# Two transformer blocks in float32 on one core: an altered matmul order at the start of the FFN down projections

## The chip, the cores and the metric
The kernel runs on one core of a Trainium2 chip. The core has a tensor engine (PE in the profile; its weight loads are PEld), a vector engine (DVE), a scalar engine (ACT), GpSimd (POOL) and SyncE (SP), which here only starts DMA transfers. The engines run their own instruction streams and wait for each other on semaphores. The metric is the device time of one execution in microseconds, as the median of several runs.

## The reference
An input of 256 tokens by 1024 features (272 tokens with 16 meta tokens in front) goes through a block of two layers (latent attention, then window pooling, each followed by a convolutional feed-forward network) and then through a second block (gated linear attention and convolution, a gated feed-forward network, an extra gate, a last norm). There are three feed-forward networks; each has an up projection and a down projection with 2816 hidden features between them:

```python
def conv_ffn(h, w_up, conv_w, conv_b, w_down):        # first block, layers 0 and 1
    L = h.shape[1]
    u = h @ w_up
    up = jnp.pad(u, ((0, 0), (CONV_WIDTH - 1, 0), (0, 0)))
    u = conv_b + sum(conv_w[j] * up[:, j:j + L] for j in range(CONV_WIDTH))
    gate, val = jnp.split(u, 2, axis=-1)
    return (jax.nn.silu(gate) * val) @ w_down
...
        a, bb = jnp.split(u2 @ w_gate_upffn[i], 2, axis=-1)   # second block
        h = h + (jax.nn.silu(a) * bb) @ w_down[i]
```

## The kernel before, in words
Every product in float32 is made of three matmuls on a high and a low part of both operands (`three`, lines 379 to 381: high by high, high by low, low by high). So each weight tile has to be split first: ACT copies `raw` to `w_high` with rounding (L752 for a first half, L755 for the rest or the whole), then DVE and POOL each subtract for their columns of `w_low` (DVE L1083 and L1088, POOL L1575, which has a quarter of the columns or a little more).

Weights come in **units**. A unit of a down projection holds the 22 tiles of 128 rows (chunks 0 to 21) that make one block of 128 output features: 22 x 3 = 66 matmuls into one PSUM bank, with 272 tokens in the first network and 256 in the other two. A down projection has eight units, 0 to 7; each network's units are called unit 0, unit 1 and so on below (`n0`, `n0 + 1` in the code). There are two slots of `raw`, `w_high` and `w_low`, so unit n+2 uses the slots of unit n: ACT may write `w_high` of unit n+2 only when PE has finished unit n (it waits for `products`), while SP may load `raw` of unit n+2 as soon as unit n has been split. In program order ACT does, after unit n's last matmul, in the first two networks the square (L771) and the copy (L796) of its output (`post`), then the high part of unit n+2 (`high`); in the third network the high part comes first. DVE and POOL follow with the low parts, and PE waits for all three counters before unit n+2 (`parts_ready`).

The moving operand of chunk k, `x_high` and `x_low`, is made during the up projection from its turn k: scaling from PSUM, convolution taps, SiLU, product, then ACT L805 (`x_high`) and DVE L1188 (`x_low`). In the first two networks the work of a turn is finished one turn later, so the last two chunks, 20 and 21, are finished after the up projection's last matmul. PE waits for each chunk of unit 0 by name (`x_ready`). Unit 1 follows unit 0; its x is the same, so it waits for no chunk. Units 2 to 7 run in a loop.

The order of the work is the order in which the code is written, engine by engine; there is no scheduler.

Of the kernel before, what the change touches and what calls it, by code (L numbers as in the profile page):

```python
# [50 lines left out]
FC = FF // P  # L51
# [69 lines left out]
FIRST_UNIT, FIRST_BLOCK, UNITS, BLOCKS = {}, {}, [], []  # L121
# [46 lines left out]
def program(nc, dram, marks, final):  # L168
    ctx = ExitStack()
    with ctx:  # L170
        def sb(name, shape, dt=F32, stack=None):
            return (stack or ctx).enter_context(nc.sbuf_tensor(name, shape, dt))

        def sem(name):
            return ctx.enter_context(nc.semaphore(name))
# [3 lines left out]
        def done(name, i=None):  # L179


            engine, n, loop = marks.get(name, ("scalar", 1, None))
            stride = marks.get(("stride", engine, loop), 1)
            if final and name not in marks:
                raise KeyError(name)
            if isinstance(i, tuple):
                i, n = i[0], n - i[1] * stride
            return step_sems[engine], n if i is None else i * stride + n

        products = sem("products")  # L190
# [40 lines left out]
        xh = sb("x_high", [P, FC, T1], F32R)  # L231
        xl = sb("x_low", [P, FC, T1], F32R)
# [33 lines left out]
        bank = [ctx.enter_context(nc.psum_tensor(f"bank{b}", [P, 512], F32)) for b in range(8)]  # L266
# [74 lines left out]
        def up_place(j):  # L341


            return (j, None) if j < 2 or j >= FC - 2 else (f"k{j % 2}", (j - 2) // 2)
# [15 lines left out]
        def _(pe):  # L360
            S = Steps("tensor", step_sems["tensor"], marks)

            def parts_ready(n, i=None):

                at = n + 1 if i is None else 2 * i + (n + 1)
                pe.wait_ge(high_parts, at)
                pe.wait_ge(low_parts_v, at)
                pe.wait_ge(low_parts_g, at)

            def bank_free(b, i=None, stride=0):  # L370

                before = BLOCKS[b]["before"]
                if before is not None:
                    x = BLOCKS[before]
                    pe.wait_ge(freed[x["eng"]], x["freed"] if i is None else i * stride + x["freed"])

            def three(out, hi, lo, rhi, rlo, start, stop):

                nc.tensor.matmul(out, hi, rhi, start=start, stop=False)  # L379
                nc.tensor.matmul(out, hi, rlo, start=False, stop=False)  # L380
                return nc.tensor.matmul(out, lo, rhi, start=False, stop=stop)  # L381

            def weights(n, j):
                return wh[n % 2][:, j * P:(j + 1) * P], wl[n % 2][:, j * P:(j + 1) * P]

            def unit(n, T, xs, chunk_ready=None, middle=None, i=None, order=None):

                U = UNITS[n]
                nb, kc = U["blocks"], U["tiles"] // U["blocks"]
                if n > 0:  # L390
                    parts_ready(n, i)
                for b in range(nb):
                    bank_free(U["first"] + b, i, 2 * nb)
                for at, k in enumerate(order or range(kc)):
                    if chunk_ready is not None:
                        chunk_ready(k)
                    if middle is not None and at == kc // 2:
                        middle()
                    for b in range(nb):
                        hi, lo = weights(n, k * nb + b)  # L400
                        last = three(bank[BLOCKS[U["first"] + b]["bank"]][:, 0:T], hi, lo,
                                     xs[0][:, k, 0:T], xs[1][:, k, 0:T], at == 0, at == kc - 1)
                        if at == kc - 1:
                            last.then_inc(products, 1)
# [66 lines left out]
            def ffn_down(l, T):  # L471
                n0 = FIRST_UNIT[f"down{l}"]

                def x_ready(j):
                    k, i = up_place(j + 1 if l < 2 else j)
                    pe.wait_ge(*done(f"x high {l} {k}", i))
                    pe.wait_ge(*done(f"x low {l} {k}", i))
                unit(n0, T, (xh, xl), x_ready)
                unit(n0 + 1, T, (xh, xl))
                with pe.Fori(0, (DC - 2) // 2) as i:  # L480
                    for k in range(2):
                        unit(n0 + 2 + k, T, (xh, xl), i=i)
# [30 lines left out]
            for half in range(2):  # L513
                for t, (q0, nq) in enumerate(QT):
                    b = UNITS[n]["first"] + half * 3 + t
                    bank_free(b)
                    out = bank[BLOCKS[b]["bank"]][0:nq, :]
                    for k in range(KC):
# [4 lines left out]
                        last = nc.tensor.matmul(out, ul[:, QC + k, toks], wh[n % 2][:, at],  # L523
                                                start=False, stop=k == KC - 1)
# [6 lines left out]
            for s in range(-1, NH + 2):  # L531
                if s + 1 < NH:
# [4 lines left out]
                    for out, (q0, nq) in ((X[0:96, 0:96], QT[0]), (X[0:96, 96:288], QT[1]), (Y[0:80, 0:T1], QT[2])):  # L537
                        last = nc.tensor.matmul(out, Q[:, g, q0:q0 + nq], K[:, g, 0:q0 + nq], start=True, stop=True)
                    last.then_inc(*S.step(f"scores {g}"))
                if s >= 2:  # L540
# [7 lines left out]
                    for c, (k0, nk) in enumerate(QT):  # L548
                        last = nc.tensor.matmul(o[:, k0:T1], V[0:nk, c, g * VD:(g + 1) * VD],
                                                PT[0:nk, g % 2, PTOFF[c]:PTOFF[c] + T1 - k0],  # L550
                                                start=c == 0, stop=c == 2)
                    last.then_inc(*S.step(f"values {g}"))
                if 1 <= s <= NH:
# [6 lines left out]
                    for out, t, c in ((bank[4][0:96, 0:96], 0, 0), (bank[4][0:96, 96:192], 1, 0),  # L560
# [4 lines left out]
                        last = nc.tensor.transpose(out, src, ident[0:nq, 0:nq])  # L565
# [10 lines left out]
            norm_rows("post0", token_rows(R_BANK, T1))  # L576
            ffn_up(0, T1, "f0")
            ffn_down(0, T1)
            norm_sums("fpost0", f"fpost0 acc {DC - 2}", squares(0, T1), True)
            norm_rows("fpost0", token_rows(R_BANK, T1))  # L580
# [5 lines left out]
            first = UNITS[n]["first"]  # L586
            parts_ready(n)
            for half in range(2):
                for t, (t0, nt_) in enumerate(TT):
                    b = first + half * len(TT) + t  # L590
                    bank_free(b)
                    for g in range(2 * half, 2 * half + 2):
                        out = bank[BLOCKS[b]["bank"]][0:nt_, (g % 2) * 256:(g % 2) * 256 + 256]
                        for k in range(2):
                            if t == 0:
# [4 lines left out]
                            last = nc.tensor.matmul(out, ul[:, 2 * g + k, toks], wh[n % 2][:, at],  # L600
                                                    start=False, stop=k == 1)
# [4 lines left out]
            for c in range(DC):  # L606
# [3 lines left out]
                b = first + 2 * len(TT) + c  # L610
                bank_free(b)
                for t, (t0, nt_) in enumerate(TT):
                    last = nc.tensor.matmul(bank[BLOCKS[b]["bank"]][:, t0:T1], pz[0:nt_, t, c * P:(c + 1) * P],
                                            wm[0:nt_, g, WIN_AT[t]:WIN_AT[t] + T1 - t0],
                                            start=t == 0, stop=t == len(TT) - 1)
                last.then_inc(products, 1)
            norm_sums("post1", f"post1 acc {DC - 2}", squares(0, T1), True)
            norm_rows("post1", token_rows(R_BANK, T1))
            ffn_up(1, SEQ + HISTORY, "f1")
            ffn_down(1, SEQ)  # L620
            norm_sums("fpost1", f"fpost1 acc {DC - 2}", squares(0, SEQ), True)
            norm_rows("fpost1", token_rows(R_BANK, SEQ))
# [27 lines left out]
            T = SEQ  # L650
# [6 lines left out]
            for pair in range(2):  # L657
                last = nc.tensor.matmul(bank[6][:, pair * SEQ:(pair + 1) * SEQ], wgu[:, pair * P:(pair + 1) * P],
                                        glr[0:16, :], start=True, stop=True)
            last.then_inc(*S.step("gate logits"))  # L660

            for v in range(2):
                n = FIRST_UNIT["gin_v"] + v
                parts_ready(n)
                for t in range(2):
                    b = UNITS[n]["first"] + t
                    bank_free(b)
                    out = bank[BLOCKS[b]["bank"]][:, 0:256]
                    for k in range(DC):
# [3 lines left out]
                        last = nc.tensor.matmul(out, ul[:, k, toks], wh[n % 2][:, at], start=False, stop=k == DC - 1)  # L673
# [50 lines left out]
            blocks_in_turn(FIRST_UNIT["pproj"], T, lambda b, k: (xh[:, 8 + k, 0:T], xl[:, 8 + k, 0:T]), 2)  # L724
            ffn_up(2, T, "f2")
            ffn_down(2, T)
            n = FIRST_UNIT["pgate"]
            unit(n, T, us, u_ready("e"))
# [1056 lines left out]
```

## Time and profile before

| | us |
|---|---|
| median of 3 runs (lowest, highest) | 1041.85 (1041.72, 1045.51) |
| the profiled execution | 1046.04 |
| its span, first to last instruction | 1044.3 |
| PE busy | 961.5 (92% of the span) |
| DVE busy | 747.4 (72%) |
| ACT busy | 503.1 (48%) |
| POOL busy | 355.9 (34%) |
| mean granted TensorE clock | 0.924 of full speed |

The profile shows one execution on the one core. Busy time of PE counts matmuls whose ends are modelled, so steps from start to start are the better measure of its pace. The three down projections are at about 348 to 420 us, 606 to 673 us and 942 to 1005 us of the span.

### The profile page before, as it was taken

To read this page: it belongs to the slowest core of one execution; us is meant where nothing else is said; L and a number is where in the kernel's file an instruction comes from. 1 tells how busy PE (TensorE), PEld (TensorE's weight loads), DVE (VectorE), ACT (ScalarE), POOL (GpSimd) and SP (SyncE) were. 2 spreads that over 40 slices of the span, in tenths; PEclk is the share of its full clock that TensorE was granted. 3 is DMA by queue.
4 is the path that set the end of the run, shared out by engine and by line. 5 is a ranking of instruction groups with operands and counts; after the bars stand their busy time and mean duration, and the time that the engine had idled before them with its cause. 6 is when DMAs were issued, how large, how long until landed. Compare 5 with 4: busy or idle time off the path is not lost.

```text
span 1044.3 us, 19995 instructions
## 1 busy us (share of the span) xinstructions
PE 961.5 (92%) x7208; PEld 911.1 (87%) x7208; DVE 747.4 (72%) x1304; ACT 503.1 (48%) x831; POOL 355.9 (34%) x226
## 2 busy tenths in 40 slices
PE   6788999799999899679999989899998999999995
PEld 6786668699999899669999989899998999999995
DVE  7657662689999722648999962477978787876566
ACT  5563333455555433455665554345345545453432
POOL 4411002522222355242222245532125433335543
PEclk9897557799999999679999999989999999999998
DMA  7223000424444444212544545424323455464531
GB/s 267 102 87 115 1 0 16 147 87 175 172 169 174 169 166 171 79 41 98 181 165 161 182 164 203 176 81 176 149 81 132 164 198 187 177 228 174 199 122 41
DMA packets 20848, 145.64 MB, mean 139 GB/s; under 512 B 2480, under 2 KB 4032, under 8 KB 5440
## 3 DMA queue, kind: packets, MB, share of 16 engines
q1 hardware_dynamic: 20800, 144.99, 38.6%
q8 instruction: 31, 0.51, 0.2%
q14 instruction: 17, 0.14, 0.0%
HBM read 143.94 MB, written 1.05 MB: 139 GB/s over the span
## 4 chain that ended last, share of the span: by engine, by line
PE 32%; DVE 11%; issue 5%; ACT 5%; ACTq 1%; DVEq 0%; POOL 0%; POOLq 0%
PE bank L379 10%; PE bank L380 9%; PE bank L381 9%; DVE conv_out L1211 3%; ACT w_high L755 2%; DVE w_low L1088 2%; ACT conv_out L824 1%; ACT w_high L752 1%; PE bank L643 1%; DVE conv_out L1448 1%; DVE gla_s_diag L1429 0%; PE bank L443 0%; PE bank L671 0%; DVE conv_out L1555 0%; PE bank L672 0%
## 5 line engine op out<-in xcount | busy, mean ns | idle before, releaser
L379 PE MATMUL bank<-u_high,w_high 128*128 128x256 f32 (+2 forms) x1472 | 432.5, 294 | 32.3 <-DVE u_low L1097 20.4
L1575 POOL TENSOR_TENSOR w_low<-raw,w_high 128x512 fp32r<-128x512 f32 (+1 forms) x121 | 279.1, 2307 | 510.5 <-ACT w_high L755 510.5
L380 PE MATMUL bank<-u_low,w_high 128*128 128x256 f32 (+2 forms) x1472 | 424.1, 288 | 0.0
L381 PE MATMUL bank<-u_high,w_low 128*128 128x256 f32 (+2 forms) x1472 | 423.3, 288 | 0.0
L379 PEld LDWEIGHTS bank<-u_high,w_high 128*128 128x128 f32 x1472 | 284.6, 193 | 44.8 <-issue 22.6
L1088 DVE TENSOR_TENSOR w_low<-raw,w_high 128x768 fp32r<-128x768 f32 (+4 forms) x120 | 213.8, 1782 | 139.9 <-ACT w_high L755 138.6
L380 PEld LDWEIGHTS bank<-u_low,w_high 128*128 128x128 f32 x1472 | 284.7, 193 | 0.0
L381 PEld LDWEIGHTS bank<-u_high,w_low 128*128 128x128 f32 x1472 | 283.9, 193 | 0.0
L755 ACT ACTIVATE w_high<-raw 128x1280 fp32r<-128x1280 f32 (+4 forms) x120 | 206.6, 1722 | 69.6 <-PE bank L381 64.1
L379 PE MATMUL bank<-x_high,w_high 128*128 128x256 f32 (+1 forms) x608 | 173.6, 285 | 11.2 <-DVE x_low L1188 4.8
L381 PE MATMUL bank<-x_high,w_low 128*128 128x256 f32 (+1 forms) x608 | 173.2, 285 | 0.0
L380 PE MATMUL bank<-x_low,w_high 128*128 128x256 f32 (+1 forms) x608 | 172.5, 284 | 0.0
L379 PEld LDWEIGHTS bank<-x_high,w_high 128*128 128x128 f32 x608 | 115.3, 190 | 13.0 <-issue 4.8
L1588 POOL TENSOR_TENSOR acc<-acc,sq 128x272 f32<-128x272 f32 (+2 forms) x84 | 70.0, 833 | 157.3 <-ACT sq L771 146.1
L380 PEld LDWEIGHTS bank<-x_low,w_high 128*128 128x128 f32 x608 | 115.2, 189 | 0.0
L381 PEld LDWEIGHTS bank<-x_high,w_low 128*128 128x128 f32 x608 | 115.0, 189 | 0.0
L1211 DVE SCALAR_TENSOR_TENSOR conv_out<-conv_in,par,conv_out 128x272 f32<-128x272 f32 (+1 forms) x176 | 87.1, 534 | 6.2 <-ACT conv_out L824 0.7
L752 ACT ACTIVATE w_high<-raw 128x768 fp32r<-128x768 f32 (+1 forms) x66 | 56.7, 859 | 60.6 <-PE bank L381 60.0
L831 ACT ACTIVATE conv_out<-conv_out 128x272 f32<-128x272 f32 (+1 forms) x44 | 18.7, 425 | 110.7 <-DVE conv_out L1211 110.7
L1083 DVE TENSOR_TENSOR w_low<-raw,w_high 128x768 fp32r<-128x768 f32 (+1 forms) x66 | 64.5, 978 | 8.6 <-ACT w_high L752 8.6
L1140 DVE TENSOR_TENSOR conv_in<-bank,r_rows 128x256 f32<-128x256 f32 (+2 forms) x140 | 54.1, 427 | 15.0 <-PE bank L381 9.6
L1097 DVE SCALAR_TENSOR_TENSOR u_low<-h,par,u_high 128x272 fp32r<-128x272 f32 (+3 forms) x56 | 54.4, 989 | 1.0 <-ACT u_high L779 1.0
(180 smaller groups left out, 958.3 us busy)
## 6 DMA issues: line engine op xcount, KB each, us to landing
raw<-w_up_dram SPq DMA_DIRECT2D x66, 1024.0 KB, 4.8
raw<-w_down_dram SPq DMA_DIRECT2D x24, 1408.0 KB, 6.0
raw<-w_gin_c_dram SPq DMA_DIRECT2D x4, 1536.0 KB, 6.7
raw<-w_wo_dram SPq DMA_DIRECT2D x4, 1024.0 KB, 4.7
raw<-w_wout_dram SPq DMA_DIRECT2D x4, 1024.0 KB, 4.9
raw<-w_pgate_dram SPq DMA_DIRECT2D x4, 1024.0 KB, 4.7
raw<-w_gin_v_dram SPq DMA_DIRECT2D x2, 1024.0 KB, 4.9
raw<-w_gin_g_dram SPq DMA_DIRECT2D x2, 1024.0 KB, 4.8
```

The costliest lines, as they stand in the source:

```text
L379: nc.tensor.matmul(out, hi, rhi, start=start, stop=False)
L380: nc.tensor.matmul(out, hi, rlo, start=False, stop=False)
L381: return nc.tensor.matmul(out, lo, rhi, start=False, stop=stop)
L752: nc.scalar.activation(wh[n % 2][:, 0:split], raw[n % 2][:, 0:split], ACT.Copy).then_inc(*S.step(first))
L755: nc.scalar.activation(wh[n % 2][:, split:cols], raw[n % 2][:, split:cols], ACT.Copy).then_inc(high_parts, 1)
L1083: nc.vector.tensor_tensor(wl[n % 2][:, 0:split], raw[n % 2][:, 0:split], wh[n % 2][:, 0:split].bitcast(F32), ALU.subtract).then_inc(*S.step())
L1088: nc.vector.tensor_tensor(wl[n % 2][:, split:cols], raw[n % 2][:, split:cols], wh[n % 2][:, split:cols].bitcast(F32), ALU.subtract).then_i ...
L1097: nc.vector.scalar_tensor_tensor(ul[:, c, 0:T], h[:, c, t0:t0 + T], pcol(gain, c), uh[:, c, 0:T].bitcast(F32), ALU.mult, ALU.subtract)\
L1140: nc.vector.tensor_tensor(out, bank[BLOCKS[b]["bank"]][:, 0:T], rows[:, 0:T], ALU.mult)\
L1211: nc.vector.scalar_tensor_tensor(cv[:, hf, 0:T], ur[:, hf, skip + tap:skip + tap + T], pcol(f"cw{l}", (tap * 2 + hf) * FC + j), cv[:, hf, ...
L1575: nc.gpsimd.tensor_tensor(wl[n % 2][:, at], raw[n % 2][:, at], wh[n % 2][:, at].bitcast(F32), ALU.subtract).then_inc(low_parts_g, 1)
L1588: nc.gpsimd.tensor_tensor(acc[:, a, 0:T], acc[:, a, 0:T], sq[:, label % 2, 0:T], ALU.add).then_inc(*step)
```

## The change
In the down projection's first two units the chunks are multiplied in another order: unit 0's chunks 0 to 19, unit 1's chunks 0 to 9, unit 0's chunks 20 and 21, unit 1's chunks 10 to 21. The waits for unit 1's weights and bank come before its chunk 0 as before, and each unit still counts up `products` behind its last matmul. No other engine's code is touched.

```diff
                     k, i = up_place(j + 1 if l < 2 else j)
                     pe.wait_ge(*done(f"x high {l} {k}", i))
                     pe.wait_ge(*done(f"x low {l} {k}", i))
-                unit(n0, T, (xh, xl), x_ready)
-                unit(n0 + 1, T, (xh, xl))
+
+                parts = ((n0, 0, FC - 2), (n0 + 1, 0, FC // 2 - 1), (n0, FC - 2, FC), (n0 + 1, FC // 2 - 1, FC))
+                for u, from_, to in parts:
+                    b = UNITS[u]["first"]
+                    if from_ == 0:
+                        parts_ready(u)
+                        bank_free(b)
+                    for k in range(from_, to):
+                        if u == n0:
+                            x_ready(k)
+                        hi, lo = weights(u, k)
+                        last = three(bank[BLOCKS[b]["bank"]][:, 0:T], hi, lo, xh[:, k, 0:T], xl[:, k, 0:T],
+                                     k == 0, k == FC - 1)
+                    if to == FC:
+                        last.then_inc(products, 1)
                 with pe.Fori(0, (DC - 2) // 2) as i:
```

On PE in the first network, where unit 0 has weights `w_high1` and bank 3 and unit 1 has `w_high0` and bank 0: the end of unit 0 and the start of unit 1 before. Each matmul that waits for a chunk of x waits for `vector_steps,scalar_steps`; the one that waits for the parts is unit 1's first.

```order
L379 MATMUL bank3<-x_high,w_high1 128x272 [waits vector_steps,scalar_steps]
L380 MATMUL bank3<-x_low,w_high1 128x272
L381 MATMUL bank3<-x_high,w_low1 128x272
L379 MATMUL bank3<-x_high,w_high1 128x272 [waits vector_steps,scalar_steps]
L380 MATMUL bank3<-x_low,w_high1 128x272
L381 MATMUL bank3<-x_high,w_low1 128x272
L379 MATMUL bank0<-x_high,w_high0 128x272 [waits low_parts_g,freed_v,low_parts_v,high_parts]
L380 MATMUL bank0<-x_low,w_high0 128x272
L381 MATMUL bank0<-x_high,w_low0 128x272
```

In the changed program, after unit 1's thirtieth matmul (chunk 9), these stand in the same queue:

```order
L379 MATMUL bank0<-x_high,w_high0 128x272
L380 MATMUL bank0<-x_low,w_high0 128x272
L381 MATMUL bank0<-x_high,w_low0 128x272
L379 MATMUL bank3<-x_high,w_high1 128x272 [waits vector_steps,scalar_steps]
L380 MATMUL bank3<-x_low,w_high1 128x272
L381 MATMUL bank3<-x_high,w_low1 128x272
L379 MATMUL bank3<-x_high,w_high1 128x272 [waits vector_steps,scalar_steps]
L380 MATMUL bank3<-x_low,w_high1 128x272
L381 MATMUL bank3<-x_high,w_low1 128x272
L379 MATMUL bank0<-x_high,w_high0 128x272
L380 MATMUL bank0<-x_low,w_high0 128x272
L381 MATMUL bank0<-x_high,w_low0 128x272
```

The six matmuls of unit 0's chunks 20 and 21, with their two waits, have moved behind 30 matmuls of unit 1. The same move of six rows stands at three places of PE's program, one in each down projection, the third one's included (`ffn_down` is one function for all three); the number of instructions is the same.

## Rows read from the trace of the kernel before

**Rows 1.** The page, part 1: busy time, share of the span, instructions.
```profile
PE 961.5 (92%) x7208; PEld 911.1 (87%) x7208; DVE 747.4 (72%) x1304; ACT 503.1 (48%) x831; POOL 355.9 (34%) x226
```

**Rows 2.** Timeline of PE, first down projection: start, length, operation, [idle before <- releaser].
```profile
355.68 0.29 PE L381 MATMUL bank<-x_high,w_low 128*128 128x272 f32 x1
...
357.39 0.37 PE L379 MATMUL bank<-x_high,w_high 128*128 128x272 f32 x1 [1.43 <-DVE x_low L1188]
...
358.88 0.36 PE L379 MATMUL bank<-x_high,w_high 128*128 128x272 f32 x1 [0.87 <-DVE x_low L1188]
...
359.21 0.29 PE L381 MATMUL bank<-x_high,w_low 128*128 128x272 f32 x1
359.33 0.29 PE L379 MATMUL bank<-x_high,w_high 128*128 128x272 f32 x1
...
369.21 0.28 PE L379 MATMUL bank<-x_high,w_high 128*128 128x272 f32 x1
...
377.48 0.29 PE L379 MATMUL bank<-x_high,w_high 128*128 128x272 f32 x1
```

**Rows 3.** Stretches: length, busy of PE, PEld, DVE, ACT, POOL, granted clock, DMA.
```profile
361.00:363.00 2.00, 2.00 (x11) 2.00 (x11) 0.14 (x1) 1.82 (x1) 0.10 (x1) 0.50 0.00 0
618.00:620.00 2.00, 2.00 (x20) 2.00 (x19) 0.00 (x0) 2.00 (x3) 0.74 (x1) 1.00 0.33 141
```

**Rows 4.** Timeline of DVE, ACT, POOL and SP, first down projection.
```profile
358.29 0.44 DVE L1188 TENSOR_TENSOR x_low<-x_full,x_high 128x272 fp32r<-128x272 f32 x1 [0.50 <-ACT x_high L805]
...
359.61 0.40 ACT L771 ACTIVATE sq<-bank 128x272 f32<-128x272 f32 x1 [1.36 <-PE bank L381]
...
352.34 2.89 POOL L1575 TENSOR_TENSOR w_low<-raw,w_high 128x768 fp32r<-128x768 f32 x1 [4.34 <-ACT w_high L755]
...
362.90 3.95 POOL L1575 TENSOR_TENSOR w_low<-raw,w_high 128x768 fp32r<-128x768 f32 x1 [1.97 <-ACT w_high L755]
...
355.47 0.33 SPq L316 DMA_DIRECT2D raw<-w_down_dram  x1
```

**Rows 5.** Timeline of PE, second down projection.
```profile
613.55 0.28 PE L381 MATMUL bank<-x_high,w_low 128*128 128x256 f32 x1
615.50 0.36 PE L379 MATMUL bank<-x_high,w_high 128*128 128x256 f32 x1 [1.67 <-DVE x_low L1188]
...
616.94 0.36 PE L379 MATMUL bank<-x_high,w_high 128*128 128x256 f32 x1 [0.84 <-DVE x_low L1188]
...
617.25 0.28 PE L381 MATMUL bank<-x_high,w_low 128*128 128x256 f32 x1
...
625.19 0.29 PE L379 MATMUL bank<-x_high,w_high 128*128 128x256 f32 x1
```

**Rows 6.** Timeline of ACT and POOL, second down projection.
```profile
617.65 0.38 ACT L771 ACTIVATE sq<-bank 128x256 f32<-128x256 f32 x1 [1.32 <-PE bank L381]
...
610.55 2.87 POOL L1575 TENSOR_TENSOR w_low<-raw,w_high 128x768 fp32r<-128x768 f32 x1 [4.27 <-ACT w_high L755]
...
620.92 3.94 POOL L1575 TENSOR_TENSOR w_low<-raw,w_high 128x768 fp32r<-128x768 f32 x1 [1.99 <-ACT w_high L755]
```

**Rows 7.** Timeline of PE and POOL, third down projection.
```profile
949.91 0.28 PE L379 MATMUL bank<-x_high,w_high 128*128 128x256 f32 x1
...
957.59 0.28 PE L381 MATMUL bank<-x_high,w_low 128*128 128x256 f32 x1
957.71 0.28 PE L379 MATMUL bank<-x_high,w_high 128*128 128x256 f32 x1
...
944.64 2.88 POOL L1575 TENSOR_TENSOR w_low<-raw,w_high 128x768 fp32r<-128x768 f32 x1 [2.87 <-ACT w_high L755]
...
952.75 3.94 POOL L1575 TENSOR_TENSOR w_low<-raw,w_high 128x768 fp32r<-128x768 f32 x1 [4.97 <-ACT w_high L755]
```

**Rows 8.** Timeline of PE: first matmul behind three other long waits.
```profile
45.45 0.56 PE L379 MATMUL bank<-u_high,w_high 128*128 128x272 f32 x1 [3.66 <-DVE m L1273]
...
69.90 0.60 PE L379 MATMUL bank<-u_high,w_high 128*128 128x272 f32 x1 [2.31 <-DVE rope_a L1297]
...
788.11 0.36 PE L379 MATMUL bank<-x_high,w_high 128*128 128x256 f32 x1 [2.48 <-ACT x_high L1029]
```

## The prediction
> **What bounds the kernel now.** The page's first part comes first: PE is busy for 92% of the span, and of the other engines DVE is the busiest with 72% [rows 1]. So what counts is when PE waits, and at what clock it works. Then the timeline of PE at the start of the first down projection [rows 2]: unit 0's chunk 19 ends with the matmul at 355.68, chunk 20 starts at 357.39 after 1.43 us idle, chunk 21 at 358.88 after 0.87 us, both behind DVE's x_low. That is the last turn of the up projection, finished late. The second network shows the same, 1.67 and 0.84 us [rows 5]. In the third, where a turn's x is finished inside the turn, unit 0 runs through: unit 1 starts at 949.91, right behind [rows 7]. So there are two holes of about 2.3 and 2.5 us for the moved matmuls to fill, and a third place with no hole.
>
> Last the clock. In the first network unit 1 needs 369.21 - 359.33 = 9.88 us for 66 matmuls, unit 2 needs 377.48 - 369.21 = 8.27 [rows 2]: unit 1 ran partly at the granted clock of 0.50, which is 1.2 GHz [rows 3], after PE had been idle twice. That cost 1.61 us on top. In the second network, after holes of the same size, the clock stayed at 1.00 [rows 3]. Step from matmul to matmul at full clock: 8.27 / 66 = 0.1253 us with 272 tokens, (957.71 - 949.91) / 66 = 0.1182 us with 256 [rows 2, 7].
>
> **What the change removes.** With 30 matmuls of unit 1 in front of chunk 20, PE reaches chunk 20 at 355.68 + 31 x 0.1253 = 359.56; the last x_low ends at 358.29 + 0.44 = 358.73 [rows 2, 4]. In the second network it reaches chunk 20 at 613.55 + 31 x 0.1182 = 617.21, and chunk 20 could start at 615.50, chunk 21 at 616.94 [rows 5]. Both holes go entirely. Unit 1's weights must now be there earlier, at 355.80 and 613.67; their last part is POOL's, which ends at 355.23 and 613.42 [rows 4, 6], 0.57 and 0.25 us before. In the third they are needed 6 matmuls sooner, at 949.2, and ready at 947.52 [rows 7]. That wait therefore costs 0; if POOL ran a little later, at most some tenths. SP, which waits for the same POOL instruction, issues its transfer at 355.47, 0.24 us behind POOL's end [rows 4], so the ends of POOL's rows can be used.
>
> **What it adds.** Not an instruction, but a longer way to the end of unit 0. And on that end hangs the weight chain of unit 2, which shares unit 0's slot: ACT waits for products, copies the high part, POOL subtracts, PE waits for POOL. In the first network it takes from unit 0's last matmul at 359.21 to POOL's end at 362.90 + 3.95 = 366.85 [rows 2, 4], 7.64 us; in the second from 617.25 to 624.86, 7.61 us [rows 5, 6]; in the third from 949.79 (949.91 less a step) to 956.69, 6.9 us [rows 7]. Before, all 66 matmuls of unit 1 lay beside this chain (7.8 us or more). Now 30 of them are used up ahead of it and only 36 are left: 4.5 or 4.3 us. PE must wait before unit 2, in all three networks. A handoff of a late operand to PE takes 358.88 - 358.73 = 0.15 us, and the first matmul after a wait 0.08 us longer (0.36 against 0.28) [rows 2, 4].
> - First network: unit 0's last matmul at 355.68 + 36 x 0.1253 = 360.19 instead of 359.21, so 0.98 later. POOL ends at 367.83, unit 2 starts in effect at 367.83 + 0.23 = 368.06, against 369.21: gain 1.15 us. PE idles from 360.19 + 36 x 0.1253 + 0.29 = 364.99 to 367.98, 3.0 us.
> - Second: last matmul at 613.55 + 36 x 0.1182 = 617.81 instead of 617.25, 0.56 later; POOL ends at 625.42, unit 2 starts in effect at 625.65 against 625.19: loss 0.46 us. Idle 3.2 us (622.07 + 0.28 to 625.57).
> - Third: there was no hole, so unit 0 ends 30 x 0.1182 = 3.55 us later. POOL ends at 956.69 + 3.55 = 960.24, unit 2 starts in effect at 960.47 against 957.71: loss 2.76 us. Idle 2.5 us (957.59 + 0.28 to 960.39).
>
> Sum without any new effect of the clock: -1.15 + 0.46 + 2.76 = +2.1 us. The gain in the first network already has the 1.61 us of its slow stretch in it. Later units keep their cover: PE starts unit 2 with unit 3's chain begun about 3 us ahead, and a chain of 7.6 us or less then lies beside 66 matmuls of 7.8 to 8.3 us, as now. The transfer for unit 4 is issued as soon as unit 2 is split, so it moves with unit 2; it takes about 6 us of the 7.8 that unit 2 runs. I cost both at 0.
>
> **The clock behind the new holes.** This is the unknown. Rows of single or paired waits in an otherwise full stream: 3.66 us restarted slow (0.56 us for a matmul), 2.31 us restarted slow (0.60), 2.48 us restarted at full clock (0.36) [rows 8]; 1.43 + 0.87 us was followed by a slow stretch, 1.67 + 0.84 us by none [rows 2, 3, 5]. So between 2.3 and 2.5 us it goes either way, at 3.66 it fell. The new holes are 3.0, 3.2 and 2.5 us, each in one piece: I take 8, 8 and 5 in 10, two falls as the likeliest count. A fall costs between 0 (it ends inside the wait) and 1.61 us; I take 1.5, near the row, as nearly nothing of the slow stretch there fell into idle time. Two falls: +3.0 us.
>
> The Trainium skill, TensorE: Matmul & The Clock Gate, section "HAM oscillation — how this bites in real kernels", describes a kernel whose wait before each tile throttles the engine again, so that every next tile starts cold. By that all three units would start slow, +6.9 us in sum; the trace here does not quite agree, since the wait of 2.48 us restarted at 0.36 us a matmul.
>
> **The sum.** +2.1 + 3.0 = +5.1 us. For a profiled execution like this one, 1046.04 (span 1044.3 and 1.7 around it), that is 1051.1. The median of the unprofiled runs lies 4.2 us lower, and its two old holes may have fallen in the clock or not, on average once in two as in the profile, which is what the sum has. So 1041.85 + 5.1 = 1046.9 us.
>
> **The rivals.**
> 1. All three new holes bring the clock down: +2.1 + 4.5 to 4.8 = 1048.4 to 1048.8. For it: 3.0 and 3.2 us are nearer to the 3.66 that fell than to any that did not. Against it: 2.48 held.
> 2. The clock holds behind two or all of them: +2.1 to +3.6, 1043.9 to 1045.5. For it: 2.48 us and the pair of 2.51 us held. Against: nothing above 2.5 us did.
> 3. Faster: unit 2's weights are there in time, so the holes are filled and no wait takes their place. First network: unit 2 would start at 355.68 + 73 x 0.1253 = 364.83, 4.4 us sooner; second 613.55 + 73 x 0.1182 = 622.18, 3.0 sooner; third 0: 1034.5. The point of decision is a chain from unit 0's last matmul to POOL's end of 4.5 us instead of 7.6. Every unit of the trace that I read has 6.9 or more, and the slot is the same one, so this is nearly excluded.
> 4. Only the two networks with holes are changed, and the third is left alone: then -0.7 and two falls, +2.3, 1044.2. The order of PE's program shows the move at three places, so it is out.
>
> **How the numbers follow.** Forecast, two falls, 0.40 (1046.9, by itself 1045.8 to 1047.8); rival 1, 0.32; rival 2, 0.23; rival 3, 0.03; anything else 0.02. What a measurement can tell from no change is 0.5%, 5.2 us: below 1036.6 is faster, above 1047.1 slower. Slower: nearly all of rival 1, 0.30, and 0.4 of the forecast, 0.16, with the rest 0.47. Faster 0.03, same 0.50. Range: from no new fall and some tenths less than the sum, 1043.4, to three falls and some tenths more, 1049.3.
>
> **What would show it.** In the changed profile: no wait for x_low at chunks 20 and 21 in the first two down projections; unit 1's first matmul in the middle of an unbroken stream; then in each of the three a wait of PE before unit 2 of 3.0, 3.2 and 2.5 us, put down to POOL's or DVE's w_low; unit 0's end to POOL's end still 7.6, 7.6 and 6.9 us; the granted clock at 0.5 behind two or three of these waits. The third down projection would be 2.8 us longer or more. The prediction is wrong if no wait stands before unit 2 (then rival 3), if the chain is shorter than I read it, or if later units lose or regain time, which I put at 0.

## The result, and the profile after

The changed kernel takes 1053.6 us (median of 8 runs, 1049.91 to 1056.02) against 1045.13 us for the kernel before in 8 runs (1041.72 to 1046.07); the ratio is 1.0078 with a 95% interval of 1.0057 to 1.0099. That is slower by about 8.1 us. The forecast was 1046.9 us with a range up to 1049.3, too low by 6.7 us. Half of that, 3.3 us, is the base: the three runs known beforehand had a median of 1041.85, the eight have 1045.13. The rest is the size of the change: 5.1 us forecast, 8.1 measured by the ratio (8.5 between the two medians).

The page after, parts 1 and 4, whose first row answers to [rows 1]:

```profile
PE 966.7 (92%) x7208; PEld 917.8 (87%) x7208; DVE 748.1 (71%) x1304; ACT 503.2 (48%) x831; POOL 355.1 (34%) x226
...
PE 78%; DVE 11%; issue 4%; ACT 3%; POOL 2%; DMA 1%; SPq 0%; POOLq 0%; DVEq 0%; ACTq 0%
```

PE is busy for 5 us more with the same 7208 matmuls: more of them ran at the lower clock, as the counts below show. The shares hide the rest, so the waits of PE are read projection by projection (who was waited for, us in total, times, longest):

```profile
PE bank L379 <- POOL w_low L1588: 3.1, 1, 3.1
PE bank L379 <- ACT w_high L768: 3.3, 1, 3.3
PE bank L379 <- POOL w_low L1588: 2.6, 1, 2.6
```

These are the largest waits inside the first, second and third down projection. No wait for x_low is left in any. The ACT named in the second is the inference from semaphore events; POOL's share of w_low ended last there too, as the timeline shows (lines of the code are 13 higher after the change). First projection, PE, ACT and POOL, in answer to [rows 2, 4]:

```profile
362.04 0.29 PE L381 MATMUL bank<-x_high,w_low 128*128 128x272 f32 x1
362.45 0.40 ACT L784 ACTIVATE sq<-bank 128x272 f32<-128x272 f32 x1 [2.52 <-PE bank L381]
363.11 2.56 ACT L768 ACTIVATE w_high<-raw 128x2816 fp32r<-128x2816 f32 x1
365.75 3.92 POOL L1588 TENSOR_TENSOR w_low<-raw,w_high 128x768 fp32r<-128x768 f32 x1 [1.97 <-ACT w_high L768]
...
366.56 0.29 PE L381 MATMUL bank<-x_high,w_low 128*128 128x272 f32 x1
369.90 0.59 PE L379 MATMUL bank<-x_high,w_high 128*128 128x272 f32 x1 [3.06 <-POOL w_low L1588]
```

Unit 0's last matmul starts at 362.04, POOL ends at 369.67: 7.63 us, as before. Unit 1 is finished at 366.85, and PE idles 3.06 us and starts again at half pace. Second and third projection, in answer to [rows 5, 6] and [rows 7]:

```profile
618.68 0.28 PE L381 MATMUL bank<-x_high,w_low 128*128 128x256 f32 x1
...
622.35 3.92 POOL L1588 TENSOR_TENSOR w_low<-raw,w_high 128x768 fp32r<-128x768 f32 x1 [2.00 <-ACT w_high L768]
626.51 0.58 PE L379 MATMUL bank<-x_high,w_high 128*128 128x256 f32 x1 [3.31 <-ACT w_high L768]
...
956.84 0.28 PE L381 MATMUL bank<-x_high,w_low 128*128 128x256 f32 x1
...
959.79 3.92 POOL L1588 TENSOR_TENSOR w_low<-raw,w_high 128x768 fp32r<-128x768 f32 x1 [8.48 <-ACT w_high L768]
963.94 0.58 PE L379 MATMUL bank<-x_high,w_high 128*128 128x256 f32 x1 [2.57 <-POOL w_low L1588]
```

The chains are 7.59 and 6.87 us long, forecast from before as 7.61 and 6.9. The granted clock behind the three waits (length, busy times of PE, PEld, DVE, ACT and POOL, clock, DMA share and rate), in answer to [rows 3]:

```profile
370.00:373.00 3.00, 3.00 (x13) 3.00 (x14) 2.33 (x1) 0.17 (x1) 3.00 (x2) 0.50 0.65 197
373.50:375.00 1.50, 1.50 (x14) 1.50 (x13) 0.00 (x0) 0.00 (x0) 0.73 (x1) 1.00 0.92 391
626.60:628.00 1.40, 1.40 (x7) 1.40 (x8) 1.40 (x1) 0.00 (x0) 1.40 (x2) 0.50 0.41 72
628.00:632.00 4.00, 4.00 (x20) 4.00 (x20) 1.11 (x1) 0.00 (x0) 2.79 (x1) 0.50 0.82 335
633.00:635.00 2.00, 2.00 (x19) 2.00 (x19) 0.00 (x0) 0.00 (x0) 0.00 (x0) 1.00 0.95 377
964.00:967.00 3.00, 3.00 (x14) 3.00 (x15) 3.00 (x3) 0.81 (x2) 3.00 (x2) 0.50 0.66 195
```

The clock fell to 1.2 GHz (0.50) behind each of the three. In the second it stayed there about twice as long.

For the comparison of kernels a projection's length is used: from the start of its first to the start of its last matmul, from PE's timeline. "Slow" counts matmuls that last over 0.40 us (0.28 or 0.29 at full clock); holes are PE's idle times inside it.

| trace | first: us, slow, holes | second | third |
|---|---|---|---|
| before | 70.53, 14, 1.43 + 0.87 | 65.57, 0, 1.67 + 0.84 | 62.44, 0, none |
| changed | 71.14, 13, 3.06 | 68.87, 27, 3.31 | 66.63, 13, 2.57 |
| first_two | 70.98, 13, 3.06 | 68.87, 27, 3.28 | 62.45, 0, none |
| third_only | 68.91, 0, as before | 65.57, 0, as before | 65.28, 0, 2.56 |
| filled | 69.65, 0, 0.26 | 66.21, 0, 0.28 | 65.32, 0, 0.27 |
| four_two | 68.49, 0, 1.55 | 67.01, 15, 1.86 | 62.45, 0, none |
| chain_short | 70.36, 16, 2.37 | 66.85, 15, 2.59 | 66.03, 15, 1.89 |
| old_holes_filled | 68.91, 0, 0.23 | 65.58, 0, 0.20 | 62.45, 0, none |
| five_third | 68.92, 0, as before | 65.57, 0, as before | 63.54, 0, 0.81 |
| short_chain_four_two | 66.68, 0, 0.14 | 63.48, 0, 0.45 | 62.37, 0, none |
| chain_only | 70.03, 14, 0.82 + 0.87 | 66.34, 14, 1.12 + 0.84 | 62.37, 0, none |
| changed_again_a | 71.08, 14, 3.06 | 68.89, 27, 3.28 | 66.67, 13, 2.57 |
| changed_again_b | 69.47, 0, 3.06 | 68.92, 27, 3.31 | 66.65, 13, 2.56 |

Between the traces of before and after the three projections differ by 0.61 + 3.30 + 4.19 = 8.1 us; the profiled executions, 1046.04 and 1054.0, by 8.0. So the sum is here. The rest of the kernel comes out even in these two traces, partly by luck: the first projection begins 1.7 us later after the change, the stretches behind the first and the second are 1.5 and 0.6 us shorter, the end is 0.2 us longer. The start varies by itself: the first down projection began at 348.21 us in the trace of before and at 346.4 to 351.7 in others, with the same code ahead of it. The stretch between the first and the second projection took 186.2 to 186.4 us in the changed kernel's three traces and in first_two, and 187.3 to 188.2 in before, third_only, five_third and old_holes_filled, which have the old order there; what gives back this 1 us was not looked into.

### The profile page after: what moved, and what is told of

The parts are those of the page before. It is cut to its first block, busy times and chain, and to the rows that moved or that the text cites. A ratio compares the mean times of both kernels' runs of the same rounds, so it can differ in the third digit from the quotient of the medians.

```text
span 1052.2 us, 19995 instructions
## 1 busy us (share of the span) xinstructions
PE 966.7 (92%) x7208; PEld 917.8 (87%) x7208; DVE 748.1 (71%) x1304; ACT 503.2 (48%) x831; POOL 355.1 (34%) x226
## 4 chain that ended last, share of the span: by engine, by line
PE 78%; DVE 11%; issue 4%; ACT 3%; POOL 2%; DMA 1%; SPq 0%; POOLq 0%; DVEq 0%; ACTq 0%
PE bank L379 22%; PE bank L380 21%; PE bank L381 21%; PE bank L562 3%; PE bank L551 2%; DVE w_low L1101 2%; ACT w_high L768 2%; PE bank L578 1%; POOL w_low L1588 1%; DVE h L1176 1%; PE bank L626 1%; PE bank L656 1%; DVE u_low L1110 1%; PE bank L428 1%; PE bank L443 1%
## 5 line engine op out<-in xcount | busy, mean ns | idle before, releaser
L379 PE MATMUL bank<-x_high,w_high 128*128 128x256 f32 (+1 forms) x608 | 176.3, 290 | 14.3 <-POOL w_low L1588 5.6
L381 PE MATMUL bank<-x_high,w_low 128*128 128x256 f32 (+1 forms) x608 | 175.6, 289 | 0.0
L380 PE MATMUL bank<-x_low,w_high 128*128 128x256 f32 (+1 forms) x608 | 175.0, 288 | 0.0
L379 PEld LDWEIGHTS bank<-x_high,w_high 128*128 128x128 f32 x608 | 118.0, 194 | 15.7 <-issue 13.0
L380 PEld LDWEIGHTS bank<-x_low,w_high 128*128 128x128 f32 x608 | 117.9, 194 | 0.0
L381 PEld LDWEIGHTS bank<-x_high,w_low 128*128 128x128 f32 x608 | 117.7, 194 | 0.0
```

## The experiments

Theory A: unit 2 may start only when the chain of its weight slot is through (unit 0's last matmul, ACT, POOL), the change ends unit 0 later relative to unit 1, and a slow stretch of the clock follows the new wait. The rivals are B, the time is spread or is drift; C, only the wait counts and the clock is a by-product; D, splitting the units costs in itself.

**first_two and third_only: one part each.**

```diff
                 parts = ((n0, 0, FC - 2), (n0 + 1, 0, FC // 2 - 1), ...
+                if l == 2:
+                    parts = ((n0, 0, FC), (n0 + 1, 0, FC))
```

This is first_two; third_only has `if l < 2:` in its place.

> The new order in the first and second network only; the third network is as before. Theory A (the slot's chain: unit 2 waits for unit 0's end, and each such wait is followed by a slow stretch of the clock): the third down projection is back at its 67.7 us from its first matmul to the next stage's wait, against 71.8 in the changed kernel; the first two stay at about 72.9 and 69 to 70 us. In all +4 us against before (+3 to +5.5), 4 us less than the changed kernel. Theory B (the extra time is spread, or comes from drift of the measurement): no clear difference from the changed kernel's +8 us.

Measured: ratio 1.0018 (1.0004 to 1.0033), about +1.9 us, 12 runs; third projection back at 62.45, the first two as in the changed kernel. The place is confirmed. The total came out below the +3 to +5.5 expected. Part of that may be the clock: three of the 12 runs, with a mean granted clock of 0.927, took 1045.6 to 1045.9 us, the other nine, at 0.918 to 0.922, took 1047.0 to 1051.4. The profiled execution is the slowest of the twelve; no trace shows where the faster ones kept their clock.

> The new order in the third network only. Theory A: +2.8 us for the wait before unit 2 and +1.5 us for a slow stretch behind it if the clock falls, so +4.2 us against before, and +2.8 in runs where it holds; the wait is 2.5 to 2.6 us and put down to POOL's w_low. Theory B: the network without holes can hide 3.5 us more in its chain, and the kernel takes the time of before.

Measured: 1.003 (1.0018 to 1.0043), +3.1 us. In its trace the wait is 2.56 us and the clock held, so the projection is 2.84 us longer. Theory B, by which the third network hides the move in its chain, is out. By the ratios the two parts make 1.9 + 3.1 = 5.0 us where the whole change made 8.1; the traces do add up (3.8 us in first_two, 2.84 here and 1.35 more where the clock falls as well, 8.0 in all), so the gap lies between executions and was not closed.

```profile
960.31 0.38 PE L379 MATMUL bank<-x_high,w_high 128*128 128x256 f32 x1 [2.56 <-POOL w_low L1590]
...
960.00:962.00 2.00, 1.69 (x14) 1.70 (x15) 2.00 (x3) 1.15 (x3) 2.00 (x3) 1.00 0.40 68
962.00:964.00 2.00, 2.00 (x19) 2.00 (x19) 2.00 (x2) 0.00 (x0) 2.00 (x1) 1.00 0.88 355
```

The first row is PE's timeline, the others are stretches behind it: same wait as in the changed kernel, clock 1.00 instead of 0.50.

**filled: the wait without the idle time.**

```diff
+                for _ in range((23, 26, 20)[l]):
+                    nc.tensor.matmul(bank[NORM_BANK][:, 0:T], xh[:, 1, 0:P], xh[:, 0, 0:T],
+                                     start=True, stop=True, skip_group_check=True)
                 with pe.Fori(0, (DC - 2) // 2) as i:
```

> The changed kernel with 23, 26 and 20 spare matmuls into an unused bank between the last matmul of unit 1 and unit 2, in the first, second and third network. They keep PE at work during the new waits and do not lengthen them; their results are read by nobody. Theory A: unit 2 starts at the same time as in the changed kernel (wait left over: 0.1 to 0.4 us), but at full clock: no slow stretch behind any of the three, 4.5 to 6 us less than the changed kernel, about +2 us against before. Theory C (the clock is a by-product, only the wait counts): no change against the changed kernel.

Measured: 1.0033 (1.0015 to 1.0051), +3.5 us, against +8.1 for the changed kernel. Timeline of PE and stretches:

```profile
367.50 0.39 PE L379 MATMUL bank<-x_high,w_high 128*128 128x272 f32 x1 [0.26 <-POOL w_low L1591]
...
367.40:370.00 2.60, 2.50 (x20) 2.51 (x21) 2.23 (x1) 0.34 (x1) 2.60 (x2) 1.00 0.58 158
625.00:630.00 5.00, 5.00 (x44) 5.00 (x44) 1.01 (x1) 0.00 (x0) 2.72 (x1) 1.00 0.83 303
960.00:963.00 3.00, 3.00 (x28) 3.00 (x27) 2.86 (x2) 0.00 (x0) 3.00 (x2) 1.00 0.92 387
```

Unit 2 starts 20.04, 19.28 and 18.47 us after its projection's first matmul, against 20.01, 19.24 and 18.44 in the changed kernel: the wait is as long, only PE is not idle in it. And the clock is at 1.00 everywhere. The projections are 1.49, 2.66 and 1.31 us shorter than in the first trace of the changed kernel: 5.5 us that the clock took, and the waits alone are the rest. That the clock is a by-product without a cost is out. The 12 runs of this kernel lie in two groups, five at 1046.6 to 1048.3 us and seven at 1050.6 to 1053.9; the trace is from the lower one, and what splits them is open.

**four_two: the holes filled, and no more.**

```diff
+                parts = ((n0, 0, FC), (n0 + 1, 0, FC))
+                if l < 2:
+                    parts = ((n0, 0, FC - 2), (n0 + 1, 0, 4), (n0, FC - 2, FC - 1), (n0 + 1, 4, 6),
+                             (n0, FC - 1, FC), (n0 + 1, 6, FC))
```

> In the first two networks four chunks of unit 1 before chunk 20 and two between chunks 20 and 21, so that the old holes are filled and unit 0 ends when it did; third network as before. Theory A: no hole above 0.3 us at chunks 20 and 21; unit 0's last matmul within 0.2 us of before; PE waits 1.4 and 1.7 us before unit 2, too short for the clock to fall; unit 2 starts 2.1 us earlier than in the profiled run of before in the first network (0.5 where before had no slow stretch) and 0.1 in the second. In all -0.5 to -2.5 us against before. Theory D (splitting the units itself costs, by changes of bank and weights): +1 us or more.

Measured: 1.0002 (0.9983 to 1.0021), no difference that can be told. The holes at chunks 20 and 21 are 0.15 us at most, the waits before unit 2 are 1.55 and 1.86 us (1.4 and 1.7 expected), and the first projection takes 68.49, 0.4 us less than 68.91. But in the second the clock fell behind 1.86 us, which I had called too short for it. That refutes the step "too short for the clock to fall". The interval alone does not exclude a cost of splitting (theory D, +1 us or more), the timeline does at its place: in the changed kernel the steps from the one unit's matmuls to the other's are 0.12 to 0.14 us in the first network, like all others. The gain is small because the chain holds unit 2 anyway, as the last pair of runs shows.

**five_third: half the dose where there was no hole.** The third network alone, with five chunks:

```diff
+                if l == 2:
+                    parts = ((n0, 0, FC - 2), (n0 + 1, 0, 5), (n0, FC - 2, FC), (n0 + 1, 5, FC))
```

> As before, but in the third network five chunks of unit 1 are multiplied between unit 0's chunks 19 and 20. Ten gave a wait of 2.57 us before unit 2. If the wait is the moved work less the 0.87 us of slack that the trace of before shows (957.71 less 956.69 and a handoff of 0.15), five give 15 x 0.118 - 0.87 = 0.9 us, and no slow stretch; the projection takes 63.4 us. If the wait were due to the reordering as such, it would stay near 2.5.

Measured (one run, 1045.82 us): wait 0.81 us, 63.54 us, clock held. The wait is the moved work less the slack.

**chain_short: the chain itself.**

```diff
+    if UNITS[n]["name"].startswith("down"):
+        return 21 * P
```

> The changed kernel, and in all down projections DVE makes 21 of a unit's 22 tiles of w_low and POOL one (16 and 6 before). In the traces POOL's share of 768 columns takes 3.95 us beside DVE's 2.29. If the wait before unit 2 is set by the slot's chain, it gets shorter by what the chain does: by 0.6 to 0.9 us in each network (to about 2.4, 2.6 and 1.9 us), and 2 us in all without the clock, more if a slow stretch falls away. If the wait is set by something else (the transfer, the bank), it stays at 3.06, 3.30 and 2.57.

Measured: 1.0001 (0.9991 to 1.0011), so 8 us less than the changed kernel; waits 2.37, 2.59 and 1.89, each 0.7 us shorter. Timeline of DVE and POOL in its first projection:

```profile
362.06 2.96 DVE L1103 TENSOR_TENSOR w_low<-raw,w_high 128x2688 fp32r<-128x2688 f32 x1 [5.61 <-ACT w_high L770]
...
362.10 3.23 POOL L1590 TENSOR_TENSOR w_low<-raw,w_high 128x128 fp32r<-128x128 f32 x1 [1.97 <-ACT w_high L770]
```

POOL's 128 columns take 3.23 us beside DVE's 2.96, hardly less than 768 columns took (3.92 beside 2.29). The waits account for 2 us of the gain; the trace had slow stretches in all three projections, 15 or 16 matmuls each, so 1.3 us more comes from the second one being about half as long. The two traces differ by 8.7 us: 3.4 in the projections, 3.5 ahead of the first one, where the programs are alike and two traces of the changed kernel itself differ by 3.0 (it begins at 349.78 and 346.73 us), 1.5 in the stretches between and 0.3 behind. Why the median of twelve runs is lower by as much is open.

**old_holes_filled: the clock in the kernel before.** Order as before, with spare matmuls at the old holes.

```diff
+                        if u == n0 and l < 2 and k >= FC - 2:
+                            for _ in range((11, 5, 13, 6)[2 * l + k - FC + 2]):
+                                nc.tensor.matmul(bank[NORM_BANK][:, 0:T], xh[:, 1, 0:P], xh[:, 0, 0:T], ...
```

> The order of the kernel before, with spare matmuls into an unused bank ahead of chunk 20 (11 and 13) and chunk 21 (5 and 6) in the first two networks. They keep PE at work in the old holes. If the clock explains that the first network's projection varies, its slow stretch is gone and it takes 68.9 to 69.1 us from first to last matmul (70.5 in the trace of before with a slow stretch, 68.9 in one without), the second 65.6 to 65.8. In all 0 to 2 us less than before. If idle time has nothing to do with it, a slow stretch comes as often as before.

Measured: 0.9991 (0.9981 to 1.0002), about 1 us less and no sure difference; projections 68.91 and 65.58, without a slow stretch. One trace without a slow stretch proves little here, since the old order has none in the first projection of third_only and five_third either. With third_only and five_third, whose first two networks are as before, three traces have the old holes with their clock at stake: one slow stretch in three in the first network, none in three in the second. A fourth, chain_only (below), has the old order with somewhat shorter holes, and a slow stretch in both.

**changed_again_a and changed_again_b: the same kernel, two more traces.**

> The changed kernel unaltered, for one more profile. Waits before unit 2 of 3.0 to 3.1, 3.3 and 2.5 to 2.6 us, as in its first trace. If the slow stretches are set by the wait alone, they are again 13, 27 and 13 matmuls long. If they depend also on where in the execution the wait happens to fall, the counts differ: 13 to 16 or 26 to 30 in the first two, 0 or 13 to 16 in the third, where a wait of 2.56 us has held the clock once.

> The same once more, for a third sample: the waits within 0.1 us, the counts of slow matmuls as in the other two if the wait alone sets them, else different in at least one network.

Measured: 1054.02 and 1049.57 us, against a median of 1046.1 for the kernel before in the same series. The waits repeat within 0.03 us. The slow counts are 14, 27, 13 and 0, 27, 13: in the second of these traces the first network kept its clock behind 3.06 us of idle time.

```profile
366.58 0.39 PE L379 MATMUL bank<-x_high,w_high 128*128 128x272 f32 x1 [3.06 <-POOL w_low L1588]
...
368.00:371.00 3.00, 3.00 (x26) 3.00 (x26) 1.22 (x1) 0.00 (x0) 2.92 (x1) 1.00 0.93 345
```

So the wait alone does not decide. The same shows in a wait that is in every one of the 13 traces, that of 2.48 us at 788.11 in the trace of before [rows 8], which kept its clock there. In the changed kernel's first trace:

```profile
791.61 0.36 PE L379 MATMUL bank<-x_high,w_high 128*128 128x256 f32 x1 [2.48 <-ACT x_high L1042]
...
791.60:793.00 1.40, 1.39 (x11) 1.40 (x12) 1.36 (x5) 0.00 (x0) 0.00 (x0) 0.97 0.00 0
793.00:796.00 3.00, 3.00 (x16) 3.00 (x15) 2.45 (x4) 0.42 (x1) 0.00 (x0) 0.50 0.02 5
```

It restarts at full pace, and 1.4 us later the clock is at 0.50. In ten of the 13 traces this wait of 2.46 to 2.48 us is followed by 14 or 15 slow matmuls, in nine of these only 0.5 to 1.7 us behind a first matmul of 0.36 us. The traces of before, five_third and chain_only are the three in which it held.

The 27 slow matmuls of the second network came in four traces of four (first_two has it too), which does not look like chance; why it is twice as long there stays open.

**short_chain_four_two and chain_only: both levers, and one.** Four and two chunks in the holes, the short chain of above, and in the first two networks ACT makes the next high part before it squares and copies:

```diff
+                        high(n0 + k + 2, i)
                         post(f"fpost{l}", 2 * i + k, n0 + k, b0 + k, f"ffn_post{l}", k, i, 2)
-                        high(n0 + k + 2, i)
...
+                        low(n0 + k + 2, i)
                         add_square(name, 2 * i + k, T, done(f"{name} sq {k}", i), k=k)
-                        low(n0 + k + 2, i)
```

> Four and two chunks of unit 1 in the old holes, third network as before, DVE makes 21 of 22 tiles of w_low in the down projections, and in the first two ACT copies the next unit's high part before it squares and copies unit n's output (POOL in the same order). If unit 2's start is the later of unit 1's end and the slot's chain, the chain is now about 6.3 us against 6.0 us of remaining work of unit 1: a wait of at most 0.6 us, no slow stretch, unit 2 starts about 1.9 us earlier than in before without a slow stretch, in the first and the second network. First projection 67 us, second 63.7, third 62.4; in all -4 to -5.5 us against before. If the chain is not what holds unit 2, it comes out as the four-and-two kernel did, at 0.

> The order of PE as before the change; only the slot's chain is shortened (DVE makes 21 of 22 tiles of w_low in the down projections, and ACT and POOL in the first two take the next unit's parts ahead of unit n's square and sum). If the gain of the four-and-two kernel with the short chain comes from both together, this one is at the time of before within 1 us, since the chain was hidden behind unit 1: projections of 68.9 (70.5 with a slow stretch), 65.5 and 62.4 us. If the short chain alone made the gain, it is 4 us or more faster.

Measured: short_chain_four_two 0.9918 (0.9902 to 0.9933), 6 runs, about 8.6 us faster than before and more than the 4 to 5.5 expected; chain_only 0.9987 (0.9972 to 1.0002), which is no sure difference. Timeline of ACT, DVE and POOL of the former in the first projection, and PE's largest wait before a unit 2, in the second:

```profile
359.21 2.56 ACT L773 ACTIVATE w_high<-raw 128x2816 fp32r<-128x2816 f32 x1 [1.28 <-PE bank L383]
...
361.81 2.96 DVE L1106 TENSOR_TENSOR w_low<-raw,w_high 128x2688 fp32r<-128x2688 f32 x1 [3.40 <-ACT w_high L773]
...
361.85 3.23 POOL L1593 TENSOR_TENSOR w_low<-raw,w_high 128x128 fp32r<-128x128 f32 x1 [8.27 <-ACT w_high L773]
...
618.03 0.38 PE L381 MATMUL bank<-x_high,w_high 128*128 128x256 f32 x1 [0.45 <-POOL w_low L1593]
```

The projections take 66.68, 63.48 and 62.37 us with no slow matmul, 3.85 and 2.1 us less than in the trace of before, or 2.2 and 2.1 us less than where the old order had no slow stretch (68.91). That is 4.3 to 6 of the 8.6 us. From the trace of before to this one the span falls by 7.4 us: 6.0 in the projections, 1.4 and 1.0 in the stretches behind the first and second, while start and end are 0.2 and 0.9 longer; the cause of what lies outside the projections is open. Most of the gain needs both: the filler moves work of unit 1 into the holes, and the short chain lets unit 2 use what that frees. In chain_only's trace the second projection took 66.34 us where 65.5 was expected, by a slow stretch behind holes of 1.12 and 0.84 us; without it, chain_only might be nearly 1 us faster.

## Why the prediction was wrong

- **The holes go, at no cost at their place.** Right: no wait for x_low remains, unit 1's earlier start waited for nothing.
- **A wait before unit 2 in all three networks.** Right, and in size: 3.0, 3.2 and 2.5 us forecast, 3.06, 3.31 and 2.57 measured in the first trace; chains 7.64, 7.61 and 6.9 forecast, 7.63, 7.59 and 6.87 measured. five_third and chain_short moved the wait by the amounts that follow from it. The third network, changed without having a hole, cost the most, as forecast.
- **The sum without the clock, +2.1 us.** A little low: the filled kernel against the trace of before gives -0.88 + 0.64 + 2.88 = +2.6 us.
- **The clock behind the new holes, "+3.0 us".** This is the step that failed: the count and the size of the slow stretches. In the first trace it is 1.49 + 2.66 + 1.31 = 5.5 us. There were three slow stretches where two were the forecast (rival 1, with 0.32, had three), and one of them was 27 matmuls long. I had bounded a fall at 1.61 us by the one stretch seen behind a hole of x_low; the second network's cost 2.66 us. The trace of before has stretches of 26 slow matmuls (from 201.56 us) and of 30 (from 679.93 us), each behind two waits in a row (2.81 and 2.21 us, 2.91 and 2.90 us); the upper bound should have come from these. Why the second network's is so long is open. With 2.6 + 5.5 the sum is 8.1 us.
- **"2.48 us held", the ground for 5 in 10 in the third network and for rival 2.** The row was read rightly, but it was one draw: the same wait was followed by a slow stretch in ten of 13 traces. And a first matmul at 0.36 us does not show that the clock holds, as the stretch can begin up to 1.7 us later. Of all 16 waits of 1.86 us or more ahead of a unit 2 in these traces, 14 were followed by a slow stretch.
- **The clock of the old holes, "on average once in two".** Not settled: one slow stretch at six such places of three traces, two at two in chain_only, where the holes are shorter. The gain of 1.15 us in the first network was taken against a trace that had it; against 68.91 us, without it, the changed order loses 0.7 us there even at full clock (69.65).
- **The base.** Three runs, two of them (1041.72 and 1041.85) below all of the 35 later ones (1042.14 to 1048.75), were taken as the median. That is 3.3 us of the miss, but not the whole of it: counted from 1045.13, the upper end of the range would be 1052.6, still below 1053.6.
- **The rule of the Trainium skill.** The Trainium skill, TensorE: Matmul & The Clock Gate, section "HAM oscillation — how this bites in real kernels", tells of a kernel in which a wait of about 3 to 5 us before each tile throttles the engine each time. For this kernel's waits of 2.56 to 3.31 us that was nearer than my count: 8 slow restarts in 9 such waits of the changed kernel's three traces. It is not without exception, as changed_again_b and third_only show.

## What to carry to other kernels

Before work is pulled forward into a hole, ask what hangs on the end of the work that it pushes back: here the slot of unit 2, whose chain of 7.6 us had been hidden by all 66 matmuls of unit 1 and was not by 36. Fill a hole with as much as it holds and no more, leave alone the place that has no hole, and shorten the chain as well (either alone gave no sure gain here): the same idea with 4 + 2 chunks and a shorter chain is 0.8% faster than before, where ten chunks are 0.8% slower. Price a wait of the tensor engine such as these (1.86 to 3.31 us, 14 of 16 followed by a slow stretch of 13 to 27 matmuls) with the stretch behind it, bound that stretch by the longest in the trace, not by the nearest, and look at the granted clock for some microseconds behind the restart, not only at the first matmul. One trace in which a wait kept its clock is one draw.

## What the hardware showed that I had not expected

- POOL's tensor_tensor seems to do little while DVE's runs: 128 columns of POOL take 3.23 us beside 2.96 us of DVE, 768 columns take 3.92 beside 2.29; in the trace of before the same operation on 512 columns takes between 1.26 and 2.88 us. No run takes DVE's part away, so this is a reading of the durations. Giving DVE 21 of 22 tiles ended the pair 0.7 us sooner.
- The clock fell behind an idle time as short as 1.86 us (four_two) and a pair of 0.82 and 0.87 us (chain_only), and held behind one of 3.06 us (changed_again_b). The same wait of 2.56 us gave both. The one of 2.48 us in all 13 traces gave a slow stretch in ten, mostly after a restart at full pace.
